# Queries of the samples as stationary operand, and the first recurrent head opened one group sooner, in a two-layer hybrid decoder step

## The reference

```python
def run_trunk(x, k_cache, v_cache, s_cache, c_cache, ...):
    for l in range(DEPTH):
        h = rms_norm(x, norm_mix[l])
        proj = h @ w_in[l]
        q, k, v, hq, hf, hi, hg, cb, cc, ch = jnp.split(proj, split_idx, axis=-1)
        a, k_new, v_new = swa_sample(q, k, v, k_cache[l], v_cache[l], attn_sink[l])   # or swa_prompt
        o, S_new = hgrn2_mixer(hq, hf, hi, hg, S0, lower_bound[l], hgrn_norm[l])
        yc, buf_new = short_conv(cc * ch, buf, conv_w[l])
        x = x + jnp.concatenate([a, o, cb * yc], axis=-1) @ w_out[l]
        h = rms_norm(x, norm_ffn[l])
        gate, up = jnp.split(h @ w_gate_up[l], 2, axis=-1)
        x = x + (jax.nn.silu(gate) * up) @ w_down[l]

def sink_attend(q, k, v, mask, sink):
    s = jnp.einsum('bnqhgd,bnshd->bnhgqs', q, k).astype(jnp.float32) * ATTN_SCALE
    s = jnp.where(mask[None, :, None, None], s, NEG_BIG)
    m = jnp.maximum(jnp.max(s, axis=-1, keepdims=True), sk)
    p = jnp.exp(s - m)
    p = p / (jnp.sum(p, axis=-1, keepdims=True) + jnp.exp(sk - m))
    return jnp.einsum('bnhgqs,bnshd->bnqhgd', p.astype(v.dtype), v)
```

## Time and profile before

| | us |
|---|---|
| median of 3 runs | 2613.02 |
| lowest, highest | 2607.78, 2615.09 |
| the profiled execution | 2616.4 |
| its span, first to last instruction | 2614.8 |
| TensorE busy in it | 2576.7 (99%) |
| vector engine busy | 1484.4 (57%) |
| scalar engine busy | 1015.0 (39%) |
| GpSimd busy | 344.1 (13%) |

### The profile page before, as it was taken

The page is one execution under the profiler, slowest core; times in us unless marked ns, Lnnn a source line. Parts: engine busy times, 40 slices in busy tenths (PEclk is TensorE's granted clock), DMA queues, the critical chain, the costliest instruction groups (busy, mean ns, idle before and its releaser), DMA issues.

```text
span 2614.8 us, 51520 instructions
## 1 busy us (share of the span) xinstructions
PE 2576.7 (99%) x19424; PEld 2536.5 (97%) x19424; DVE 1484.4 (57%) x2054; ACT 1015.0 (39%) x1409; POOL 344.1 (13%) x285
## 2 busy tenths in 40 slices
PE   8999999999999999999999999999999999999997
PEld 8999999999999999999999999999999999999997
DVE  5467787555554455555555776875555444555555
ACT  5344554433333333333333535543333333333333
POOL 2011113111110011111100111131111000111111
PEclk9999999999999999999999999999999999999998
DMA  6445444544455544544454444444444545444543
GB/s 224 154 139 170 149 141 145 172 163 163 160 169 161 167 155 166 171 161 167 160 161 156 166 147 141 141 161 161 160 162 167 177 153 173 161 163 160 169 161 124
DMA packets 115724, 419.97 MB, mean 161 GB/s; under 512 B 13376, under 2 KB 14656, under 8 KB 115584
## 3 DMA queue, kind: packets, MB, share of 16 engines
q1 hardware_dynamic: 109152, 397.72, 45.8%
q0 software_dynamic: 3472, 14.04, 1.5%
q10 hardware_dynamic: 3024, 7.16, 0.7%
HBM read 411.06 MB, written 11.87 MB: 162 GB/s over the span
## 4 chain that ended last, share of the span: by engine, by line
PE 96%; DVE 2%; POOL 1%; ACT 1%; issue 0%; DMA 0%; DVEq 0%; SPq 0%; ACTq 0%; POOLq 0%
PE gp L1424 31%; PE gp L1426 30%; PE gp L1425 30%; PE mb L1468 1%; PE mb L1579 1%; PE mb L1600 0%; PE mb L1592 0%; POOL acc L1352 0%; PE mb L1477 0%; PE mb L1567 0%; PE mb L1538 0%; DVE rstd L724 0%; PE mb L1634 0%; DVE wlo L699 0%; DMA raw<-wstream 0%
## 5 line engine op out<-in xcount | busy, mean ns | idle before, releaser
L1424 PE MATMUL gp<-xh,whi 128*128 128x288 f32 x4096 | 1228.2, 300 | 12.9 <-DVE xl L1123 9.8
L1425 PE MATMUL gp<-xl,whi 128*128 128x288 f32 x4096 | 1211.9, 296 | 0.0
L1426 PE MATMUL gp<-xh,wlo 128*128 128x288 f32 x4096 | 1208.0, 295 | 0.0
L699 DVE TENSOR_TENSOR wlo<-raw,whi 128x1024 fp32r<-128x1024 f32 x754 | 971.1, 1322 | 345.6 <-ACT whi L410 342.0
L410 ACT ACTIVATE whi<-raw 128x1024 fp32r<-128x1024 f32 x754 | 769.0, 1052 | 578.6 <-PE gp L1426 539.7
L1424 PEld LDWEIGHTS gp<-xh,whi 128*128 128x128 f32 x4096 | 771.5, 188 | 25.1 <-issue 24.1
L1426 PEld LDWEIGHTS gp<-xh,wlo 128*128 128x128 f32 x4096 | 774.5, 189 | 0.0
L1425 PEld LDWEIGHTS gp<-xl,whi 128*128 128x128 f32 x4096 | 772.6, 189 | 0.9
L1424 PE MATMUL gp<-fh,whi 128*128 128x288 f32 x1408 | 416.7, 296 | 0.0
L1425 PE MATMUL gp<-fl,whi 128*128 128x288 f32 x1408 | 415.4, 295 | 0.0
L1426 PE MATMUL gp<-fh,wlo 128*128 128x288 f32 x1408 | 414.0, 294 | 0.0
(11 more groups left out here) (249 smaller groups left out, 1868.1 us busy)
## 6 DMA issues: line engine op xcount, KB each, us to landing
raw<-wstream SPq DMA_DIRECT2D x754, 512.0 KB, 4.2
s<-s_cache POOLq DMA_DIRECT2D x8, 512.0 KB, 9.8
hs_out<-s ACTq DMA_DIRECT2D x8, 512.0 KB, 2.8
caches_out<-caches POOLq DMA_DIRECT2D x8, 496.0 KB, 8.0
x<-x_in ACTq DMA_DIRECT2D x4, 576.0 KB, 8.7
y_out<-x SPq DMA_DIRECT2D x4, 576.0 KB, 2.8
kct<-kt_cache POOLq DMA_DIRECT2D x4, 512.0 KB, 6.5
vct<-v_cache POOLq DMA_DIRECT2D x4, 512.0 KB, 7.2
```

Of the source, the lines that this page charges most:

```text
L699: v.tensor_tensor(wlo[slot][:], raw[slot][:], whi[slot][:].bitcast(F32), ALU.subtract).then_inc(lo_ready, 1)
L1424: t.matmul(out, w_hi, mv_hi, start=first, stop=False)
L1425: t.matmul(out, w_hi, mv_lo, start=False, stop=False)
L1426: mm = t.matmul(out, w_lo, mv_hi, start=False, stop=last)
```

## The change

**Scores.** `qs` becomes 128 x 8 x 32: for each sample, 16 columns of key head 0 (nonzero in partitions 0 to 63) and 16 of key head 1 (partitions 64 to 127), zero elsewhere. GpSimd clears it in each round (step "qs0"); in round gg = 0 it first waits for the stores of the last head, since the tile now reaches into their buffer. TensorE takes a sample's 32 columns as stationary operand, four samples in four column groups, and lets the cached keys (128 columns) and the new keys (32 columns) move. The scores come out with queries in partitions, and the copies to `sst` and the transposes go. The rows of the score tile are in another order (sample, key head, query), so masks and sinks are rearranged: five small vector operations in `half_masks` of layer 0, and one clearing of `new_mask` at the start.

**Opening.** The last round of the projection loop (tiles 12 to 15) is written out on the scalar and the vector engine. The three sigmoids wait for tiles 0 to 7 alone (`gates_in`), and stand behind the first `hi` of that round; masks and opening stand ahead of and behind its first two `lo`.

```diff
@@ -160,6 +160,9 @@
         own = sb("own", [TWICE, 4])
         qz = sb("qz", [P, DEC_BATCH, SAMP])
         half_mask = {i: sb(f"half_mask{i}", [P, P // (2 * HALVES[i])]) for i in MASKED}
+        new_mask = sb("new_mask", [P, 3, SAMP // 2])
+        sink_s = sb("sink_s", [P, 2 * DEPTH])
+        kv_row = sb("kv_row", [P, 2])
...
-        qs = sub(t, "qs", [P, DEC_BATCH, 4, DEC_SEQ])
-        sst = sub(t, "sst", [P, 2, P])
+        qs = sub(t, "qs", [P, DEC_BATCH, 2 * 4 * DEC_SEQ])
+        assert t[0] <= temp[0] + 15360
+        t[0] = temp[0] + 15360
...
-        ap_ = Steps(sem("attn_gpsimd"), [f"cos{n}" for n in ROPE_ORDER] + ["vst", "stored"])
+                                        "pT3", "ah3", "ses", "pts", "sah"])
+        ap_ = Steps(sem("attn_gpsimd"), [f"cos{n}" for n in ROPE_ORDER] + ["vst", "qs0", "stored"])
         at = Steps(sem("attn_tensor"), [f"R{n}" for n in ROPE_ORDER]
                    + ["sc0", "tv", "sc1", "pt0", "pv0", "sc2", "pt1", "pv1", "sc3", "pt2", "pv2", "pt3", "pv3"]
-                   + ["st", "ss", "pts", "pvs"])
+                   + ["st", "pts", "pvs"])
...
+
+        def gates_in(l):
+            return l * GROUPS + (HI // 2 + 2)
...
                 a.wait_ge(av.sem, av.at(T, "rot3"))
+                a.wait_ge(ap_.sem, ap_.at(T, "qs0"))
                 for g in range(2):
                     for i in range(4):
                         half = 64 * (i % 2)
-                        m = a.activation(qs[64 * g:64 * g + 64, :, i, :], qg[half:half + 64, 2 * g + i // 2, SEQ:TOK]
+                        at_ = 16 * g + DEC_SEQ * i
+                        m = a.activation(qs[64 * g:64 * g + 64, :, at_:at_ + DEC_SEQ], qg[half:half + 64, 2 * g + i // 2, SEQ:TOK]
                                          .rearrange("p (b t) -> p b t", t=DEC_SEQ), ACT.Copy)
                 m.then_inc(aa.sem, aa.step("qs"))
...
-                a.wait_ge(at.sem, at.at(T, "st"))
-                a.activation(sst[:, 0, :], mb[0][:, 0:P], ACT.Copy)
-                a.activation(sst[:, 1, :], mb[1][:, 0:P], ACT.Copy).then_inc(aa.sem, aa.step("sst"))
...
-                with a.Fori(1, 4) as i:
+                with a.Fori(1, 3) as i:
                     group(n4 + i * 2, 0, 8)
-                a.wait_ge(group_out, hgrn_in(l))
-                sigmoids(l * HG_HEADS, 0, lambda name: None)
+                opening = sigmoids(l * HG_HEADS, 0, lambda name: a.wait_ge(
+                    group_out, hgrn_in(l) if name == "sig_g" else gates_in(l)))
+                group(n4 + 6, 0, 1)
+                for _ in range(3):
+                    next(opening)
+                group(n4 + 6, 1, 7)
+                next(opening)
...
                     for i in range(2):
-                        m = v.tensor_copy(own[64 * i:64 * i + SAMP, :], const(C_VM)[0:SAMP, 4 * i:4 * i + 4])
+                        v.tensor_copy(own[64 * i:64 * i + SAMP, :], const(C_VM)[0:SAMP, 4 * i:4 * i + 4])
+                    pair = const(C_MN).rearrange("p (g k j) -> p g k j", k=2, j=DEC_SEQ)
+                    v.tensor_tensor(new_mask[:, 1, :].rearrange("p (g j) -> p g j", j=DEC_SEQ), pair[:, :, 0, :],
+                                    pair[:, :, 1, :], ALU.max)
+                    for k in range(2):
+                        m = v.tensor_reduce(kv_row[:, k:k + 1], pair[:, :, k, 0], AX.X, ALU.max)
+                    m.then_inc(masks_made, 1)
+                    v.wait_ge(masks_made, 1)
+                    sinks = par[:, P_AT[P_SS]:P_AT[P_SS] + 4 * DEPTH].rearrange("p (t k) -> p t k", k=2)
+                    v.tensor_scalar(sink_s[:], sinks[:, :, 0], kv_row[:, 0:1], None, ALU.add).then_inc(masks_made, 1)
+                    v.wait_ge(masks_made, 2)
+                    m = v.scalar_tensor_tensor(sink_s[:], sinks[:, :, 1], kv_row[:, 1:2], sink_s[:], ALU.add, ALU.max)
                 m.then_inc(masks_made, 1)
-                v.wait_ge(masks_made, l + 1)
+                v.wait_ge(masks_made, l + 3)
...
-                v.wait_ge(at.sem, at.at(T, "ss"))
-                for g in range(2):
-                    v.scalar_tensor_tensor(ss[:, g, 0:WINDOW], mb[0][:, 256 + g * P:256 + (g + 1) * P], ATTN_SCALE,
-                                           const(C_MC), ALU.mult, ALU.add)
-                    m = v.scalar_tensor_tensor(ss[:, g, WINDOW:], mb[g][:, P:P + SAMP],
-                                               ATTN_SCALE, const(C_MN), ALU.mult, ALU.add)
+                v.wait_ge(at.sem, at.at(T, "st"))
+                v.scalar_tensor_tensor(ss[:, :, 0:WINDOW], mb[0][:, 0:2 * P].rearrange("p (r s) -> p r s", r=2), ATTN_SCALE,
+                                       const(C_MC).unsqueeze(1).to_broadcast([P, 2, WINDOW]), ALU.mult, ALU.add)
+                for r in range(2):
+                    m = v.scalar_tensor_tensor(ss[:, r, WINDOW:], mb[0][:, 2 * P + r * SAMP:2 * P + (r + 1) * SAMP],
+                                               ATTN_SCALE, new_mask[:, 1 - r:3 - r, :].rearrange("p b j -> p (b j)"),
+                                               ALU.mult, ALU.add)
...
-                sink = par[:, bass.ds(P_AT[P_SS] + T * 2, 2)]
-                v.tensor_tensor(sts[:, 5, :], sts[:, 0, :], sink, ALU.max).then_inc(av.sem, av.step("smm"))
+                v.tensor_scalar(sts[:, 5, :], sts[:, 0, :], sink_s[:, T:T + 1], None, ALU.max).then_inc(av.sem, av.step("smm"))
...
-                with v.Fori(1, 4) as i:
+                with v.Fori(1, 3) as i:
                     in_groups(i)
                 v.wait_ge(const_loaded, 16)
-                v.wait_ge(ones_set, 5)
+                v.wait_ge(ones_set, 6)
                 half_masks(l)
-                v.wait_ge(group_out, hgrn_in(l))
+                group(n4 + 6, 0, 2)
                 opening(l * HG_HEADS, 0)
+                group(n4 + 6, 2, 2)
+                used(n4 + 6, 4)
+                out_proj(0, 12)
+                group(n4 + 6, 4, 4)
+                used(n4 + 6, 8)
+                out_proj(1, 14)
...
+            e.memset(new_mask[:], NEG_BIG).then_inc(ones_set, 1)
...
+                if gg == 0:
+                    hgrn_stored(e, l)
+                e.memset(qs[:], 0.0).then_inc(ap_.sem, ap_.step("qs0"))
                 e.wait_ge(av.sem, av.at(T, f"rot{ROPE_ORDER[-1]}"))
...
+                e.wait_ge(aa.sem, aa.at(T, "qs"))
...
-                for b in range(DEC_BATCH):
-                    for g in range(2):
-                        rows = slice(64 * g, 64 * g + 64)
-                        t.matmul(mb[g][:, 16 * b:16 * b + 16], kct[gg][rows, b, :],
-                                 qs[rows, b, :, :].rearrange("p i t -> p (i t)"), start=True, stop=True)
-                for g in range(2):
-                    rows = slice(64 * g, 64 * g + 64)
-                    mm = t.matmul(mb[g][:, P:P + SAMP],
-                                  qs[rows, :, :, :].rearrange("p b i t -> p (b i t)"), krg[rows, SEQ:TOK],
-                                  start=True, stop=True)
+                for r in range(2):
+                    for keys in (kct[gg], None):
+                        for g in range(4):
+                            b, rows = 4 * r + g, slice(32 * g, 32 * g + 32)
+                            if keys is not None:
+                                t.matmul(mb[0][rows, r * P:(r + 1) * P], qs[:, b, :], keys[:, b, :], start=True, stop=True)
+                            else:
+                                at_ = 2 * P + r * SAMP
+                                mm = t.matmul(mb[0][rows, at_:at_ + SAMP], qs[:, b, :], krg[:, SEQ:TOK],
+                                              start=True, stop=True)
                 mm.then_inc(at.sem, at.step("st"))
                 yield
-                t.wait_ge(aa.sem, aa.at(T, "sst"))
-                for g in range(2):
-                    mm = t.transpose(mb[0][:, 256 + g * P:256 + (g + 1) * P], sst[:, g, :], ident)
-                mm.then_inc(at.sem, at.step("ss"))
                 yield
                 yield
                 t.wait_ge(av.sem, av.at(T, "sp"))
-                for g in range(2):
-                    t.transpose(mb[2][:, g * P:(g + 1) * P], ss[:, g, 0:WINDOW], ident)
-                    mm = t.transpose(mb[2][0:SAMP, 256 + g * P:256 + (g + 1) * P], ss[:, g, WINDOW:], ident)
+                for r in range(2):
+                    t.transpose(mb[2][:, r * P:(r + 1) * P], ss[:, r, 0:WINDOW], ident)
+                    mm = t.transpose(mb[2][0:SAMP, 256 + r * P:256 + (r + 1) * P], ss[:, r, WINDOW:], ident)
```

More of the change, by code:

```diff
@@ L336, in build @@
         aa = Steps(sem("attn_scalar"), ["krx", "qs", "es0", "kvt", "pT0", "es1", "ah0", "pT1", "es2", "ah1", "pT2", "es3", "ah2",
-                                        "pT3", "ah3", "sst", "ses", "pts", "sah"])
-        ap_ = Steps(sem("attn_gpsimd"), [f"cos{n}" for n in ROPE_ORDER] + ["vst", "stored"])
+                                        "pT3", "ah3", "ses", "pts", "sah"])
```

(21 more changed lines are left out.)

## The result

The changed kernel takes 2590.39 us (median of four runs, 2589.65 to 2590.64) beside 2613.78 us before (2607.78 to 2615.09). The ratio is 0.9918, with a 95% interval of 0.9904 to 0.9932: 0.8% faster. The forecast was 2592.5 us and "faster". The profiled execution is 2590.64 us where that of before was 2616.4 us, 25.8 us less; 23.9 us had been worked out.

What follows compares the result with a forecast made beforehand. TensorE bounds the kernel, busy 2576.7 of 2614.8 us. Opening 13.0 us plus four rounds of 2.7 us (scores 1.0, transposes 0.2, clock 1.5), 10.9 us, make 23.9 us: 2616.4 us becomes 2592.5 us, range 2586 to 2600.

Steps and rivals of the forecast that it cites:

- The opening, 13.0 us: First head of each layer: opening sooner removes TensorE's wait and the low clock behind it, 2 x 6.50 us.
- The cover: Last projection round: masks and opening delay a pair of wlo, yet slabs stay ready with a least lead of 2.0 us.
- The scores, 1.0 us a round: Samples' score block in four rounds: 2.12 us becomes 1.1 us, with short records priced no dearer than long ones.
- the prediction's other estimate, 0.4 us: New score block: 16 short records at about 60 cycles each at least, making the sum 0.2 us a round lower.
- The transposes, 0.2 us: Behind the scores in each round: two transposes removed, with the slower start of the next slab, 0.2 us saved.
- The clock, 1.5 us a round: Slab behind the samples' scores: 24 matmuls take 4.68 us instead of 3.17; the whole 1.51 us goes, bounds 0 and 1.51.
- Half as long and four groups: Reasons for no fall behind the scores: the new block is half the old one's length and fills four column groups.
- Added elsewhere, nothing: GpSimd clears qs in each round, 0.32 us, before the scalar engine writes it: cost nothing, cover 1.6 us.
- the slower rival: GpSimd's clearing waits for the last head's stores, scalar engine waits, TensorE starves: over 2620.8 us, 1%.
- Serial column groups: Rival in the new score block: column groups run one after the other, 2.5 us a block, 2598.1 us, 5%.
- Falls behind the new block: Rival: the clock still falls behind the new scores or elsewhere in the same slab, 2598.5 us, 12%.
- The opening did what it should: Denies the rival that head 0 waits for the next thing, so the 13.0 us stay: 2605.5 us, 4%.

Runs made afterwards that it cites:

- e1: Kernel before with only the earlier opening of head 0, scores as before: 2598.0 us beside 2610.08 us, ratio 0.9946.
- e2: Changed kernel with masks and opening back behind the whole projection loop, so only the new scores: 2600.19 us beside 2610.08 us, ratio 0.9958.
- e4: Changed kernel with the new score block run three times over in each round, same result: 2595.38 us (one run).
- e3: Changed kernel with all eight samples' score matmuls sent to one column group, samples' outputs wrong: 2597.36 us (one run).
- e8: Changed kernel without the new-key score matmuls of samples 0 to 3, their outputs wrong: 2591.52 us (one run).
- e6: Kernel before with each cached-key score matmul moving 128 query columns instead of 16, samples' scores wrong: 2608.52 us beside 2610.79 us, ratio 0.9988.
- e7: Kernel before with the cached-key scores of samples 1, 3, 5 and 7 left out: 2604.88 us beside 2610.79 us, ratio 0.9975.
- e11: Early opening with the old scores, cached-key matmuls written twice in a row: 2610.97 us beside 2614.27 us for the kernel before, ratio 0.9990.
- e5: Changed kernel with head 0's opening ahead of the first pair of wlo of its round instead of behind it: 2590.93 us for the changed kernel's 2590.39.
- e9: Changed kernel with the samples' value matmuls, cached and new, written twice in a row, same result: 2596.1 us.
- e10: Changed kernel with the samples' cached-value matmuls run four times in a row, samples' outputs wrong: 2606.24 us (nine runs, a tenth left out).

## Why the prediction was right

**The bound.** Right. Shares first, then waits, then the clock by stretches: only what TensorE itself did or waited for moved the time.

**The opening, 13.0 us.** 34.90 us in head 0, the value of the other heads: 6.50 us in layer 0 as forecast. Comparing equal iterations gave wait and low clock in one number, and e1 confirms it alone. But it was the price in that execution. In e2's, the wait was 1.0 us shorter in all and the low clock behind it half as long, and the two layers together cost 3.2 us less. The cover was right too: small mask operations 1.0 us (1.2 taken), pair of wlo from 95.76 (96.0), opening 98.04 to 100.5 (at most 3.4 us; it took 2.5), lead 2.0 us. Of the 0.9 us between, one operation has nearly all: L772 took 1.33 us before, and 0.45 us in its new place (L796). GpSimd's gate product ran beside it before, from 123.39 to 124.20 us, and nothing of GpSimd ran beside the new one; that this is the reason was not tried.

**The scores, 1.0 us a round.** Too small: 2.12 - 0.70 = 1.42 us. The step that was off is "the eight with 32 columns are no dearer than that, so at most 1.14 us", from which I took 1.1 and gave "1.0" as the low end. L1527 gave the right price for the long records (0.56 us in e4 for a block with everything in it). The short ones were priced at 36 ns too. But 36 ns is about what a short record takes when the column groups do not overlap (31 ns in e3), and e8 shows 8 ns each in four groups. All 16 add 0.13 us to the 0.57 of the long ones; the prediction's other estimate, 0.4 us for them, was too large as well. The low end was taken from records on 64 stationary columns, which is another form. Four rounds: 1.7 us too little, all of the difference between 23.9 and the 25.6 us below.

**The transposes, 0.2 us.** Right: 72 projection matmuls without a break where a run of 24 and one of 48 stood, with 0.27 us from the last start of one to the first of the other.

**The clock, 1.5 us a round.** Right in effect: none of the four falls is left. The reason given (few moving columns) holds in e6, and e7 and e11 add the length. "Half as long and four groups" gave two reasons more; in e3 and e4, one run each, the clock stayed at 1.00 without the second and without the first. But the full 6.0 us are the price against an execution in which all four rounds fell, and more than half of the runs of before had probably two falls there at most.

**Added elsewhere, nothing.** GpSimd clears qs in 0.31 us at 268.30 us (its timeline of after), and the scalar engine writes it from 270.33 us on (its own timeline, same execution):

```profile
268.30 0.31 POOL L1355 MEMSET qs<- 128x256 f32 x1
```

```profile
270.33 1.90 ACT L552 ACTIVATE qs<-qg 64x32 f32<-64x32 f32 x8 [4.14 <-DVE qg L977]
```

The scalar engine waited for the vector engine's qg there, not for GpSimd, so the slower rival did not come about; the cover is 1.7 us for the 1.6 forecast.

**The sum.** 13.0 + 4 x (1.42 + 0.22 + 1.51) = 25.6 us, measured 25.8 between the profiled executions. The median of before is lower than its profiled execution by 2.6 us, and I had guessed that this spread is falls of the clock. Its runs bear that out. In one set of 13 the mean granted clock is 0.995 to 0.996 for the six from 2607.5 to 2609.0 us, 0.994 to 0.995 from 2609.1 to 2610.5 us, and 0.992 for the three from 2614.7 to 2616.2 us. The changed kernel has 0.997 in every run and a spread of 1 us, and so have e5 and e9, with the same block and four runs each. So the change saves about 26 us where before was unlucky and 17 us where it was lucky, and the 23.4 us between the medians is one draw of that.

**The other rivals.** Serial column groups would have cost 2.37 us a block (e3; 2.5 worked out). Falls behind the new block did not appear at three times its length either, in the one run of e4. The opening did what it should (e1). The rule that gaps without matmuls lower the clock (the Trainium skill, "TensorE: Matmul & The Clock Gate", HAM oscillation) would, taken alone, have left the four falls. It fits the waits ahead of head 0, with which the clock fell in both layers. Behind the scores the trace had spoken against it, and e6, which has as few gaps as the kernel before and no falls there, settles it for this kernel.

What stays open: which measure of activity the chip takes. Moving columns and length decide between e6, e7, e11 and the kernel before; why value matmuls with the same 16 columns showed no fall in e9 and one in four rounds in e10 would need more forms. Whether a block of given length falls depends on something that differs from run to run, which was not tried. In the seven falls of the kernel before and e1 the clock fell 2.3 to 3.4 us after the block's first record, so the block's place in time may matter beside its kind and length; e6 and e7 had ten runs each, e3 and e4 one.

## What to carry to other kernels

In a kernel that TensorE bounds, look at the granted clock by stretches even where the engine has no wait: a block with few moving columns per stationary load can cost nearly as much again in the slab behind it as it takes itself (here 1.5 us behind 2.1). Look at the spread of the runs beside it: the profiled execution may be the unlucky one or the lucky one. Where a small operand can be either, make it the stationary one in column groups and let the long one move. And price an edit by comparing equal iterations with and without the disturbance, which holds the wait and its after-effects in one number.

## What the runs showed of the hardware that I had not expected

- Widening the moving operand of a 64 x 128 stationary load from 16 to 128 float32 columns cost nothing: 2.13 us for the block either way (e6).
- 32-column records among 128-column ones in four column groups cost 8 ns each (e8), and 31 ns in one group (e3), and the whole block of 32 records takes 0.56 us when repeated (e4), against 2.37 us in one group (e3).
- The same program has runs 9 us apart on an otherwise quiet core, through how many falls of TensorE's clock it meets and how long they last; without the blocks and waits behind which it fell the spread is 1 us.
